# Weights of a two-block transformer kernel laid out unit behind unit in DRAM

## The chip, the core and the metric

The kernel runs on one core of a Trainium2 chip. The metric is the device time of one execution in microseconds (us), from the first to the last instruction.

## What is computed

Two blocks of a transformer run on 256 tokens of width 1024, all in fp32, one behind the other. The first block has two layers: a gated linear attention mixer and a mixture of experts, then a differential attention and a second mixture of experts (4 groups of 4 experts, 512 wide inside). The second block has two layers of feed-forward (2816 wide), a mixer (short convolution, gMLP, sparse attention) and feed-forward again. The parts that matter here are the products with weights:

```python
h = x @ w_in                                   # 1024 x 3088, GLA
for e in range(MOE_EXPERTS):                   # 16 experts, twice
    hdn = silu(t @ w_gate[e]) * (t @ w_up[e])  # 1024 x 512 each
    y = y + combine[:, e:e + 1] * (hdn @ w_down[e])
q1, q2 = split(x @ w_q); kv = x @ w_kv         # 1024 x 1024, 1024 x 2048
swiglu(x, w_gate, w_up, w_down)                # 1024 x 2816, 2816 x 1024, four times
```

Each weight is read from DRAM once. Some 400 MB of weights go through the core in one execution.

## The kernel before

**Units.** All weights are cut into units: up to four rows of k (128 partitions each) by 512 columns, or eight by 256, 1 MB, 2048 fp32 elements for each partition. Some units are smaller: the first product (`q`) has units of two rows of k (512 KB), `kw` has four rows of 280 columns, the low-rank product one unit of 64 KB, the last units of `fdown` two rows. `plan`, `plan_cols`, `plan_split`, `plan_moe` and `plan_ffn` (L308 to L352) make the list `units` with a DRAM view for each unit, and `jobs`, which names the units of each product. L358 to L380 set the order.

**From DRAM to TensorE.** `load_units` (L440) issues one DMA for each unit from the SP queue into one of seven buffers `raw` of 8 KB for each partition. `round_units` (L408, ScalarE, L416) rounds a unit to fp32r into one of four buffers `Whi`. `rest_units` (L420, VectorE, L428; GpSimd L436 for six units) writes the rest `raw - Whi` over `raw` in place and calls it `Wlo`. `use_unit` (L448, TensorE) does three matmuls for each row of k and token tile: high by high (L479), rest by high (L482), high by rest (L487).

**What sets the order.** Every engine runs a program written out by hand. SP waits until unit i-7 is used before it loads unit i; ScalarE waits until unit i has landed and unit i-4 is used. Products on 256 tokens use a unit for two token tiles. The experts of a group work on one tile of 128 gathered tokens, so there a unit is used in half the time. An overflow branch (`over_steps`, L1908) loads the expert weights once more, from GpSimd's queue, if a group has more than 128 tokens.

**In DRAM** the weights lie as the reference has them: row k, then columns. A unit's part for one partition is then four runs of 512 columns (2 KB each), 128 rows of the matrix apart. For the 256-column units of `b_w_q` and `kv_w` it is eight runs of 1 KB, for `kw` four of 1120 bytes. `x_turned` (the tokens, turned and tiled on the host) lies with 4 KB in a row for each partition.

The first product has its own order: SP fetches `x0` (the first half of `x_turned`), the four `q` units, then `x1`, then the rest (L3149 to L3156).

```python
def load_units(sp, a, b):
    for i in range(a, b):
        ap, m, n, _, _ = units[i]
        if i >= NR:
            sp.wait_ge(*on("used", i - NR))
        sp.dma_start(raw[:, i % NR, 0:m * n].rearrange("p (t n) -> p t n", n=n), ap)...
```

Of the kernel before, what the change touches and what calls it, by code (L numbers as in the profile page):

```python
# [18 lines left out]
C_OWN = 1608  # L19
C_SUM = 1616  # L20
C_N = 1640


def constant_table():

    import numpy as np
    t = np.zeros((128, C_N), np.float32)
    i = np.arange(128)
# [104 lines left out]
def build(nc, A, cst_d, out):  # L133
# [14 lines left out]
    def at_(name, shape, dt, off):  # L148
        return nc.alloc_sbuf_tensor_at(name, shape, dt, offset=off)

    def take(nbytes):
        o = base[0]
        base[0] += (nbytes + 31) // 32 * 32
        return o
# [11 lines left out]
    B_o = take(8192)  # L166
    cst_o = take(C_N * 4)

# [11 lines left out]
    gb = at_("gb", [128, 2, 1024], f32, gb_o)  # L180
    cst = at_("cst", [128, C_N], f32, cst_o)

# [90 lines left out]
    where, tenant, held, order, left = {}, {}, set(), list(range(8)), {}  # L273
# [31 lines left out]
    units = []  # L305
    jobs = {}

    def plan(name, view, nk, n, per=None):  # L308

        per = per or max(1, min(nk, 2048 // n))  # L310
        js = []
        k = 0
        while k < nk:
            m = min(per, nk - k)
            js.append(len(units))
            units.append((view[:, k:k + m, :], m, n, k, nk))
            k += m
        jobs[name] = js

    def rows(ap):  # L320
        return ap.rearrange("(t p) n -> p t n", p=128)

    def plan_cols(name, ap, a, b, per=None):
        v = rows(ap)
        plan(name, v[:, :, a:b], v.shape[1], b - a, per)

    def plan_split(name, ap, order=(0, 4)):

        v = rows(ap)
        jobs[name] = [len(units) + i for i in range(4)]  # L330
        for k in order:
            for c in (0, 512):
                units.append((v[:, k:k + 4, c:c + 512], 4, 512, k, 8))

    def plan_moe(l):
        for g in range(4):
            for j in range(4):
                plan_cols(("gate", l, g, j), A["moe_w_gate"][l, 4 * g + j], 0, 512)
                plan_cols(("up", l, g, j), A["moe_w_up"][l, 4 * g + j], 0, 512)
            v = A["moe_w_down"][l, 4 * g:4 * g + 4].rearrange("e (t p) n -> p (e t) n", p=128)  # L340
            for hf in range(2):
                plan(("down", l, g, hf), v[:, :, 512 * hf:512 * hf + 512], 16, 512)

    CH = [(0, 512), (512, 1024), (1024, 1536), (1536, 2048), (2048, 2560), (2560, 2816)]

    def plan_ffn(a, l):
        for c, b in enumerate(CH[:5]):
            plan_cols(("fgate", a, l, c), A[f"{a}_gate_2"][l], *b)
            plan_cols(("fup", a, l, c), A[f"{a}_up_2"][l], *b)
        plan_cols(("fboth", a, l), A[f"{a}_both"][l], 0, 512)  # L350
        for hf in range(2):
            plan_cols(("fdown", a, l, hf), A[f"{a}_down_2"][l], 512 * hf, 512 * hf + 512)  # L352

    GLA_J = [("q", 0, 512), ("lr", 3072, 3088), ("v0", 1024, 1536), ("v1", 1536, 2048), ("k", 512, 1024),
             ("r0", 2048, 2560), ("r1", 2560, 3072)]
    MIX_J = [("kv", 1792, 2304), ("q", 1280, 1792), ("kw", 2304, 2584), ("uv", 768, 1280),
             ("ca", 0, 512), ("cb", 512, 768)]
    for n, a, b in GLA_J:  # L358
        if n == "lr":
            plan(("gla", n), A["low_rank"], 8, 16)  # L360
        else:
            plan_cols(("gla", n), A["a_w_in"][0], a, b, 2 if n == "q" else None)
    plan_split(("gla", "out"), A["a_w_out"][0])
    plan_moe(0)
    for j in range(2):
        c = 256 * j
        plan_cols(("df", 0, j), A["b_w_q"][0], c, c + 256)
        plan_cols(("df", 1, j), A["b_w_q"][0], 512 + c, 768 + c)
        plan_cols(("df", 2, j), A["kv_w"], c, c + 256)
        plan_cols(("df", 3, j), A["kv_w"], 512 + c, 768 + c)  # L370
    for j in range(2):
        plan_cols(("df", "v", j), A["kv_w"], 1024 + 512 * j, 1536 + 512 * j)
    plan_split(("df", "out"), A["b_w_out"][0])
    plan_moe(1)
    for l in range(2):
        plan_ffn("ffn1", l)
        for n, a, b in MIX_J:
            plan_cols(("mx", l, n), A["w_in_2"][l], a, b, 4 if n == "kw" else None)
        plan_split(("mx", l, "out"), A["w_out_2"][l], (4, 0))
        plan_ffn("ffn2", l)  # L380
    NU = len(units)
# [1526 lines left out]
    def over_steps(l):  # L1908

        for g in range(4):  # L1910
            for j in range(4):
                for kind in ("gate", "up"):
                    v = rows(A[f"moe_w_{kind}"][l, 4 * g + j])
                    for k in (0, 4):
                        yield (kind, g, j), v[:, k:k + 4, :], k, 8
            v = A["moe_w_down"][l, 4 * g:4 * g + 4].rearrange("e (t p) n -> p (e t) n", p=128)
            for hf in range(2):
                for k in range(0, 16, 4):
                    yield ("down", g, hf), v[:, k:k + 4, hf * 512:hf * 512 + 512], k, 16

    def over_before(lane, l, v):

# [11 lines left out]
    def overflow_pool(pool, l, place):  # L1934
        P = OVER[l]
        pool.wait_ge(*on("flag", l))
        met = dict(pool.met)
        with pool.taken(flag[0:1, 0:1], f"over{l}_pool", place):
            over_before(pool, l, V_OF[l])
            for i, (name, v, k, nk) in enumerate(over_steps(l)):  # L1940
                if i > 0:
                    pool.wait_ge(*on(P.name, "olo", i - 1))
                pool.dma_start(oraw[:, :].rearrange("p (t n) -> p t n", n=512), v).then_inc(
                    over_landed[l], tick(over_landed[l], P.name, "oraw", i, by=16))
            over_behind(pool, l)
        pool.met = met

    def overflow_act(act, l, place):
        P = OVER[l]
        act.wait_ge(*on("flag", l))  # L1950
        met = dict(act.met)
        with act.taken(flag[0:1, 0:1], f"over{l}_act", place):
            over_before(act, l, V_OF[l])
            for i, (name, v, k, nk) in enumerate(over_steps(l)):
                g = name[1]
                if k == 0 and name == ("gate", g, 0):
                    gather_act(act, P, g, 0)
                    place_turn_act(act, P, g)
                act.wait_ge(*on(P.name, "oraw", i))
                if i > 0:  # L1960
                    act.wait_ge(*on(P.name, "omm", i - 1))
                act.activation(ohi[:, :], oraw[:, :], ACT.Copy).then_inc(P.act, tick(P.act, P.name, "ohi", i))
                if k + 4 == nk and name[0] == "gate":
                    gate_act(act, P, g, name[2], where[(P.name, "out", *name)], (P.name, "out", *name),
                             on(P.name, "omm", i))
                if k + 4 == nk and name[0] == "up":
                    h_turn_act(act, P, g, name[2], ohTh[:, 4 * name[2]:4 * name[2] + 4, :])
                if k + 4 == nk and name[0] == "down":
                    act.wait_ge(*on(P.name, "omm", i))
                    act.wait_ge(*on(P.name, "scat", g - 1, 1, 1) if g else (None, 0))  # L1970
                    act.activation(oY[:, name[2] * 512:name[2] * 512 + 512],
                                   PS[where[(P.name, "out", *name)]][:, :], ACT.Copy).then_inc(
                        P.act, tick(P.act, P.name, "yg", g, name[2]))
                    free(P.act, P.name, "out", *name)
            over_behind(act, l)
        act.met = met
# [1322 lines left out]
```

## Time and profile before

| | |
|---|---|
| median of 3 runs | 1848.53 us (1848.28 to 1849.69) |
| profiled execution, span | 1848.9 us (the profile lists no other time of it) |
| TensorE matmuls (PE) | 1831.4 us busy, 99% |
| weight loads (PEld) | 1524.3 us, 82% |
| VectorE (DVE) | 1301.4 us, 70% |
| ScalarE (ACT) | 1021.1 us, 55% |
| GpSimd (POOL) | 108.5 us, 6% |
| DMA | 426.54 MB, mean 231 GB/s |

A busy TensorE is matmuls in its pipeline; their ends are modelled. "Idle before" in a row names what the engine waited for. A DMA share is the part of a stretch in which packets were under way, as a mean over the core's 16 DMA engines; it can come out a little over 1. The granted clock is the TensorE clock as a share of 2.4 GHz. "To landing" is the time from a DMA's issue to its last byte.

### The profile page before, as it was taken

The numbers are of one execution on the slowest core, as the hardware profiler recorded it, in microseconds if no ns is written. First come the engines' busy times: TensorE is split into PE (matmuls) and PEld (weight loads), VectorE is DVE, ScalarE is ACT, GpSimd is POOL, SyncE is SP. The second block draws the span as 40 slices with busy tenths as digits, with TensorE's granted clock in tenths as the row PEclk, the third lists the DMA queues.
The fourth block names the chain that finished last, engine by engine and source line by source line (L and its number), as shares of the span: only waits on it lengthen the run. The fifth ranks groups of instructions, "written<-read, shape, count | busy, mean of one in ns | idle before, by whom it ended". The sixth has DMA issues, their size and how long they took to land.

```text
span 1848.9 us, 21500 instructions
## 1 busy us (share of the span) xinstructions
PE 1831.4 (99%) x8934; PEld 1524.3 (82%) x8934; DVE 1301.4 (70%) x1335; ACT 1021.1 (55%) x1096; POOL 108.5 (6%) x105
## 2 busy tenths in 40 slices
PE   9999999999999999999999999999999999999998
PEld 7788888888978888887888888888888888888886
DVE  5479999987779999997555667655465546776544
ACT  6548777775757777774443374544254424735432
POOL 1030000000010000000000301100010003020000
PEclk9999999999999999999999999999999999999999
DMA  9548999996447999996555733655565556346551
GB/s 349 171 163 292 355 371 358 355 365 223 137 137 270 356 371 356 358 371 216 184 190 173 231 127 102 227 190 177 171 228 184 180 182 221 114 147 209 190 171 57
DMA packets 216360, 426.54 MB, mean 231 GB/s; under 512 B 7592, under 2 KB 20144, under 8 KB 216256
## 3 DMA queue, kind: packets, MB, share of 16 engines
q1 hardware_dynamic: 210448, 406.93, 63.6%
q0 software_dynamic: 5808, 18.17, 3.1%
q8 instruction: 72, 1.18, 0.3%
q14 instruction: 32, 0.26, 0.0%
HBM read 424.01 MB, written 1.06 MB: 230 GB/s over the span
## 4 chain that ended last, share of the span: by engine, by line
PE 94%; DVE 4%; DMA 1%; ACT 1%; issue 0%; POOL 0%; SPq 0%; ACTq 0%; DVEq 0%
PE ps L487 27%; PE ps L479 26%; PE ps L482 25%; PE ps L609 2%; PE ps L471 2%; PE ps L472 2%; PE ps L2628 1%; DVE Wlo L428 1%; PE ps L1703 1%; PE ps L2529 1%; PE ps L589 1%; PE ps L588 1%; PE ps L587 1%; PE ps L2116 1%; PE ps L2614 1%; DMA raw<-in_kv_w 1%
## 5 line engine op out<-in xcount | busy, mean ns | idle before, releaser
L428 DVE TENSOR_TENSOR Wlo<-raw,Whi 128x2048 fp32r<-128x2048 f32 (+2 forms) x387 | 865.1, 2242 | 400.7 <-ACT Whi L416 400.3
L416 ACT ACTIVATE Whi<-raw 128x2048 fp32r<-128x2048 f32 (+2 forms) x393 | 735.9, 1878 | 470.2 <-PE ps L487 462.3
L487 PE MATMUL ps<-Whi,XTl 128*128 128x512 f32 (+2 forms) x1440 | 536.3, 385 | 0.1
L479 PE MATMUL ps<-Whi,XTh 128*128 128x512 f32 (+2 forms) x1280 | 500.4, 391 | 0.7 <-DVE Wlo L428 0.5
L482 PE MATMUL ps<-Wlo,XTh 128*128 128x512 f32 (+2 forms) x1280 | 494.5, 386 | 0.0
L487 PEld LDWEIGHTS ps<-Whi,XTl 128*128 128x128 f32 x1440 | 269.2, 189 | 53.6 <-DVE XTl L621 0.6
L479 PEld LDWEIGHTS ps<-Whi,XTh 128*128 128x128 f32 x1280 | 241.8, 189 | 49.8 <-issue 3.1
L482 PEld LDWEIGHTS ps<-Wlo,XTh 128*128 128x128 f32 x1280 | 241.9, 189 | 45.9 <-issue 0.2
L479 PE MATMUL ps<-Whi,hTh 128*128 128x512 f32 x352 | 137.6, 391 | 0.0
L487 PE MATMUL ps<-Whi,hTl 128*128 128x512 f32 x352 | 137.1, 389 | 0.0
L482 PE MATMUL ps<-Wlo,hTh 128*128 128x512 f32 x352 | 137.0, 389 | 0.0
L479 PE MATMUL ps<-Whi,mo_hTh 128*128 128x512 f32 x256 | 100.9, 394 | 0.0
L479 PE MATMUL ps<-Whi,XGh 128*128 128x512 f32 x256 | 100.8, 394 | 0.0
L487 PE MATMUL ps<-Whi,XGl 128*128 128x512 f32 x256 | 99.8, 390 | 0.0
L487 PE MATMUL ps<-Whi,mo_hTl 128*128 128x512 f32 x256 | 99.8, 390 | 0.0
L482 PE MATMUL ps<-Wlo,mo_hTh 128*128 128x512 f32 x256 | 99.7, 390 | 0.0
L482 PE MATMUL ps<-Wlo,XGh 128*128 128x512 f32 x256 | 99.7, 389 | 0.0
L487 PEld LDWEIGHTS ps<-Whi,hTl 128*128 128x128 f32 x352 | 66.1, 188 | 13.8
L482 PEld LDWEIGHTS ps<-Wlo,hTh 128*128 128x128 f32 x352 | 66.1, 188 | 13.5
L479 PEld LDWEIGHTS ps<-Whi,hTh 128*128 128x128 f32 x352 | 66.1, 188 | 13.4
L740 POOL TENSOR_TENSOR rs<-rs,cst 128x1 f32<-128x1 f32 x16 | 24.5, 1530 | 891.6 <-DVE rs L713 891.6
L617 ACT ACTIVATE XTh<-ps 128x512 fp32r<-128x512 f32 (+1 forms) x44 | 23.9, 577 | 75.4 <-PE ps L609 75.2
(364 smaller groups left out, 2033.5 us busy)
## 6 DMA issues: line engine op xcount, KB each, us to landing
raw<-in_moe_w_gate SPq DMA_DIRECT2D x64, 1024.0 KB, 5.5
raw<-in_moe_w_up SPq DMA_DIRECT2D x64, 1024.0 KB, 6.0
raw<-in_moe_w_down SPq DMA_DIRECT2D x64, 1024.0 KB, 6.3
raw<-in_ffn_gate SPq DMA_DIRECT2D x40, 1024.0 KB, 5.1
raw<-in_ffn_up SPq DMA_DIRECT2D x40, 1024.0 KB, 5.1
raw<-in_ffn_down SPq DMA_DIRECT2D x40, 1024.0 KB, 5.0
raw<-in_w_in SPq DMA_DIRECT2D x18, 1024.0 KB, 5.4
raw<-in_a_w_in SPq DMA_DIRECT2D x10, 1024.0 KB, 13.9
```

The lines of the kernel that those rows point to most:

```text
L416: act.activation(Whi[:, i % NS, 0:m * n], raw[:, i % NR, 0:m * n], ACT.Copy).then_inc(w_rounded, tick(w_rounded, "rounded", i))
L428: dve.tensor_tensor(Wlo[:, i % NR, 0:m * n], raw[:, i % NR, 0:m * n], h.bitcast(f32), ALU.subtract).then_inc(w_rest, tick(w_rest, "rest", i))
L471: pe.matmul(o, xh(k0 + q, t), h[:, q, :], start=k0 + q == first, stop=False)
L472: pe.matmul(o, xh(k0 + q, t), l[:, q, :], start=False, stop=False)
L479: pe.matmul(o, xh(k, t), h[:, q, :], start=k == first, stop=False)
L482: pe.matmul(o, xh(k, t), l[:, q, :], start=False, stop=False)
L487: x = pe.matmul(o, xl(k, t), h[:, q, :], start=False, stop=k == end)
L587: pe.matmul(o, h[:, q, c], XTh[:, q, :], start=q == 0, stop=False)
L588: pe.matmul(o, h[:, q, c], XTl[:, q, :], start=False, stop=False)
L609: x = pe.transpose(PS[b][:, q * 128:(q + 1) * 128], blk, cst[:, C_ID:C_ID + 128])
L617: act.activation(dst, src, ACT.Copy).then_inc(act_done, tick(act_done, "hi", *name))
L740: pool.tensor_tensor(rs[:, t, 1:2], rs[:, t, 0:1], cst[:, C_ONE + 1:C_ONE + 2], ALU.pow).then_inc(pool_done, tick(pool_done, "root", v, t))
```

## The change

The host lays out each weight unit behind unit, and within a unit partition behind partition, so that one partition's part of a unit is a single run: 8 KB for a 1 MB unit, 4 KB for the `q` units and the last `fdown` units, 4480 bytes for `kw`. `by_units` does this on the host; `unit_of` makes the view of a unit from an offset in the flat array. The units, their order, sizes, buffers and waits are the same. The overflow branch uses the same arrays by the new view. The core of the diff:

```diff
+def by_units(w, a, b, per=None):
+    import numpy as np
+    lead, nk = w.shape[:-2], w.shape[-2] // 128
+    v = w[..., a:b].reshape(*lead, nk, 128, b - a)
+    per = per or unit_rows(nk, b - a)
+    return np.concatenate([np.moveaxis(v[..., k:k + per, :, :], -3, -2).reshape(*lead, -1)
+                           for k in range(0, nk, per)], axis=-1)
...
-    def plan(name, view, nk, n, per=None):
-        per = per or max(1, min(nk, 2048 // n))
+    def plan(name, flat, nk, n, per=None):
+        per = per or unit_rows(nk, n)
...
-            units.append((view[:, k:k + m, :], m, n, k, nk))
+            units.append((unit_of(flat, 128 * k * n, m, n), m, n, k, nk))
...
-    def rows(ap):
-        return ap.rearrange("(t p) n -> p t n", p=128)
+    def unit_of(flat, at, m, n):
+        return flat[at:at + 128 * m * n].rearrange("(p t n) -> p t n", p=128, n=n)
...
-                plan_cols(("gate", l, g, j), A["moe_w_gate"][l, 4 * g + j], 0, 512)
+                plan(("gate", l, g, j), A["moe_w_gate"][l, 4 * g + j], 8, 512)
...
-        plan_cols(("df", 0, j), A["b_w_q"][0], c, c + 256)
+        plan(("df", 0, j), A["b_w_q"][j], 8, 256)
...
-                    for k in (0, 4):
-                        yield (kind, g, j), v[:, k:k + 4, :], k, 8
+                    for k in (0, 4):
+                        yield (kind, g, j), unit_of(v, 65536 * k, 4, 512), k, 8
```

The same is done for `a_w_in`, `a_w_out`, `kv_w`, `b_w_out`, `moe_w_up`, `moe_w_down`, the feed-forward weights, `w_in_2` and `w_out_2`.

## Rows read from the trace of the kernel before

**Rows 1.** The page's head and its busy table (busy us, share, count).
```profile
span 1848.9 us, 21500 instructions
...
PE 1831.4 (99%) x8934; PEld 1524.3 (82%) x8934; DVE 1301.4 (70%) x1335; ACT 1021.1 (55%) x1096; POOL 108.5 (6%) x105
```

**Rows 2.** Windows: length; busy PE, PEld, DVE, ACT, POOL; clock, DMA share, GB/s.
```profile
580.00:840.00 260.00, 260.00 (x1186) 215.35 (x1185) 237.93 (x143) 193.27 (x135) 0.00 (x0) 1.00 1.00 361
860.00:1040.00 180.00, 180.00 (x822) 149.51 (x821) 95.06 (x76) 71.47 (x57) 7.73 (x3) 1.00 0.57 187
```

**Rows 3.** Waits in 580:840, the longest: who, for whom, us, times, longest.
```profile
ACT Whi L416 <- PE ps L487: 45.5, 66, 1.7
```

**Rows 4.** Unit loads (line 445) issued in 580:820, time to landing.
```profile
DMA to landing us min/median/max: 5.1/6.5/7.9
```

**Rows 5.** Waits of ScalarE over the whole span, those for unit loads.
```profile
ACT Whi L416 <- DMA raw<-in_a_w_in: 4.0, 7, 1.5
...
ACT Whi L416 <- DMA raw<-in_b_w_q: 2.8, 2, 1.7
...
ACT Whi L416 <- DMA raw<-in_kv_w: 1.1, 1, 1.1
```

**Rows 6.** Timeline at the start: start us, us, what, idle before and releaser.
```profile
7.79 1.06 ACT L416 ACTIVATE Whi<-raw 128x1024 fp32r<-128x1024 f32 x1 [0.92 <-DMA raw<-in_a_w_in]
...
10.17 0.73 PE L463 MATMUL ps<-Wlo,XTh 128*128 128x512 f32 x2
10.46 1.07 ACT L416 ACTIVATE Whi<-raw 128x1024 fp32r<-128x1024 f32 x1 [0.26 <-DMA raw<-in_a_w_in]
...
11.80 1.15 ACT L634 ACTIVATE XTh<-xs 128x512 fp32r<-128x512 f32 x2 [0.28 <-DMA xs<-in_x_turned]
```

**Rows 7.** DMA issues on the page: count, KB each, median us to landing.
```profile
raw<-in_b_w_q SPq DMA_DIRECT2D x4, 1024.0 KB, 9.8
```

**Rows 8.** Timeline where the expert stages end, first layer, then second.
```profile
417.92 0.39 PE L487 MATMUL ps<-Whi,mo_hTl 128*128 128x512 f32 x1
...
418.50 0.57 ACT L1829 ACTIVATE Ygh<-ps 128x512 fp32r<-128x512 f32 x1
...
840.07 0.39 PE L487 MATMUL ps<-Whi,mo_hTl 128*128 128x512 f32 x1
...
840.49 0.60 ACT L1829 ACTIVATE Ygh<-ps 128x512 fp32r<-128x512 f32 x1 [0.74 <-PE ps L487]
```

**Rows 9.** The mixers of the second block: one window, then matmuls of the timeline.
```profile
1562.00:1574.00 12.00, 12.00 (x73) 11.88 (x72) 4.70 (x5) 6.50 (x13) 0.00 (x0) 0.72 0.26 88
...
1067.50 0.75 PE L2529 MATMUL ps<-mx_kpe,mx_w1v 128*128 128x30 f32 x6
...
1073.71 0.48 PE L479 MATMUL ps<-Whi,XTh 128*128 128x512 f32 x1
...
1563.73 0.75 PE L2529 MATMUL ps<-mx_kpe,mx_w1v 128*128 128x30 f32 x6
...
1573.10 0.48 PE L479 MATMUL ps<-Whi,XTh 128*128 128x512 f32 x1
...
1082.16 0.35 PE L2598 MATMUL ps<-mx_kh,mx_qs 128*128 128x256 f32 x1 [0.52 <-DVE mx_kl L2938]
...
1086.59 0.40 PE L479 MATMUL ps<-Whi,XTh 128*128 128x512 f32 x1
...
1580.81 0.36 PE L2598 MATMUL ps<-mx_kh,mx_qs 128*128 128x256 f32 x1
1583.44 0.39 PE L487 MATMUL ps<-Whi,XTl 128*128 128x512 f32 x1
1583.67 0.39 PE L479 MATMUL ps<-Whi,XTh 128*128 128x512 f32 x1
```

**Rows 10.** DMA packets in 1 to 3.5 us, and the SP queue's on the page.
```profile
DMA packets 157, 0.55 MB, mean 219 GB/s; under 512 B 11, under 2 KB 11, under 8 KB 157
...
q1 hardware_dynamic: 210448, 406.93, 63.6%
```

More of the change, by code:

```diff
@@ L21, with unit_rows @@
 C_N = 1640
+GLA_J = [("q", 0, 512, 2), ("lr", 3072, 3088, None), ("v0", 1024, 1536, None), ("v1", 1536, 2048, None),
+         ("k", 512, 1024, None), ("r0", 2048, 2560, None), ("r1", 2560, 3072, None)]
+MIX_J = [("kv", 1792, 2304, None), ("q", 1280, 1792, None), ("kw", 2304, 2584, 4), ("uv", 768, 1280, None),
+         ("ca", 0, 512, None), ("cb", 512, 768, None)]
+def unit_rows(nk, n):
+    return max(1, min(nk, 2048 // n))
+def by_units(w, a, b, per=None):
[3 more added lines that the diff above has]
+    per = per or unit_rows(nk, b - a)
+    return np.concatenate([np.moveaxis(v[..., k:k + per, :, :], -3, -2).reshape(*lead, -1) for k in range(0, nk, per)],
+                          axis=-1)
 def constant_table():
@@ L315, in plan, with plan_split @@
             js.append(len(units))
-            units.append((view[:, k:k + m, :], m, n, k, nk))
+            units.append((unit_of(flat, 128 * k * n, m, n), m, n, k, nk))
             k += m
         jobs[name] = js
-    def rows(ap):
-        return ap.rearrange("(t p) n -> p t n", p=128)
[L323 to L329, printed above, removed]
+    def unit_of(flat, at, m, n):
+        return flat[at:at + 128 * m * n].rearrange("(p t n) -> p t n", p=128, n=n)
+    def plan_split(name, flat, order=(0, 4)):
         jobs[name] = [len(units) + i for i in range(4)]
         for k in order:
-            for c in (0, 512):
-                units.append((v[:, k:k + 4, c:c + 512], 4, 512, k, 8))
+            for c in range(2):
+                units.append((unit_of(flat, (k // 4 + 2 * c) * 262144, 4, 512), 4, 512, k, 8))
     def plan_moe(l):
@@ L337, in plan_moe @@
             for j in range(4):
-                plan_cols(("gate", l, g, j), A["moe_w_gate"][l, 4 * g + j], 0, 512)
-                plan_cols(("up", l, g, j), A["moe_w_up"][l, 4 * g + j], 0, 512)
-            v = A["moe_w_down"][l, 4 * g:4 * g + 4].rearrange("e (t p) n -> p (e t) n", p=128)
+                plan(("gate", l, g, j), A["moe_w_gate"][l, 4 * g + j], 8, 512)
+                plan(("up", l, g, j), A["moe_w_up"][l, 4 * g + j], 8, 512)
             for hf in range(2):
-                plan(("down", l, g, hf), v[:, :, 512 * hf:512 * hf + 512], 16, 512)
+                plan(("down", l, g, hf), A["moe_w_down"][l, g, hf], 16, 512)
     CH = [(0, 512), (512, 1024), (1024, 1536), (1536, 2048), (2048, 2560), (2560, 2816)]
     def plan_ffn(a, l):
[L347 to L350, printed above, removed]
+        for c in range(5):
+            plan(("fgate", a, l, c), A[f"{a}_gate_2"][l, c], 8, 512)
+            plan(("fup", a, l, c), A[f"{a}_up_2"][l, c], 8, 512)
+        plan(("fboth", a, l), A[f"{a}_both"][l], 8, 512)
         for hf in range(2):
[L352 to L362, printed above, removed]
+            plan(("fdown", a, l, hf), A[f"{a}_down_2"][l, hf], 22, 512)
+    for n, a, b, per in GLA_J:
+        plan(("gla", n), A[f"a_w_in_{n}"], 8, b - a, per)
     plan_split(("gla", "out"), A["a_w_out"][0])
@@ L365, in build @@
     for j in range(2):
-        c = 256 * j
-        plan_cols(("df", 0, j), A["b_w_q"][0], c, c + 256)
-        plan_cols(("df", 1, j), A["b_w_q"][0], 512 + c, 768 + c)
-        plan_cols(("df", 2, j), A["kv_w"], c, c + 256)
-        plan_cols(("df", 3, j), A["kv_w"], 512 + c, 768 + c)
+        plan(("df", 0, j), A["b_w_q"][j], 8, 256)
+        plan(("df", 1, j), A["b_w_q"][2 + j], 8, 256)
+        plan(("df", 2, j), A["kv_k"][j], 8, 256)
+        plan(("df", 3, j), A["kv_k"][2 + j], 8, 256)
     for j in range(2):
-        plan_cols(("df", "v", j), A["kv_w"], 1024 + 512 * j, 1536 + 512 * j)
+        plan(("df", "v", j), A["kv_v"][j], 8, 512)
     plan_split(("df", "out"), A["b_w_out"][0])
@@ L376, in build @@
         plan_ffn("ffn1", l)
-        for n, a, b in MIX_J:
-            plan_cols(("mx", l, n), A["w_in_2"][l], a, b, 4 if n == "kw" else None)
+        for n, a, b, per in MIX_J:
+            plan(("mx", l, n), A[f"w_in_2_{n}"][l], 8, b - a, per)
         plan_split(("mx", l, "out"), A["w_out_2"][l], (4, 0))
@@ L1912, in over_steps @@
                 for kind in ("gate", "up"):
-                    v = rows(A[f"moe_w_{kind}"][l, 4 * g + j])
+                    v = A[f"moe_w_{kind}"][l, 4 * g + j]
                     for k in (0, 4):
-                        yield (kind, g, j), v[:, k:k + 4, :], k, 8
-            v = A["moe_w_down"][l, 4 * g:4 * g + 4].rearrange("e (t p) n -> p (e t) n", p=128)
+                        yield (kind, g, j), unit_of(v, 65536 * k, 4, 512), k, 8
             for hf in range(2):
+                v = A["moe_w_down"][l, g, hf]
                 for k in range(0, 16, 4):
-                    yield ("down", g, hf), v[:, k:k + 4, hf * 512:hf * 512 + 512], k, 16
+                    yield ("down", g, hf), unit_of(v, 65536 * k, 4, 512), k, 16
     def over_before(lane, l, v):
@@ L3264 @@
     inputs["x_turned"] = x[0].reshape(2, 128, 8, 128).transpose(0, 3, 2, 1)
-    inputs["low_rank"] = inputs["a_w_in"][0][:, 3072:].reshape(8, 128, 16).transpose(1, 0, 2)
+    for n, a, b, per in GLA_J:
+        inputs[f"a_w_in_{n}"] = by_units(inputs["a_w_in"][0], a, b, per)
+    for n, a, b, per in MIX_J:
+        inputs[f"w_in_2_{n}"] = by_units(inputs["w_in_2"], a, b, per)
+    kv_w, b_w_q = inputs.pop("kv_w"), inputs.pop("b_w_q")[0]
+    del inputs["a_w_in"], inputs["w_in_2"]
+    inputs["b_w_q"] = np.stack([by_units(b_w_q, c, c + 256) for c in range(0, 1024, 256)])
+    inputs["kv_k"] = np.stack([by_units(kv_w, c, c + 256) for c in range(0, 1024, 256)])
+    inputs["kv_v"] = np.stack([by_units(kv_w, c, c + 512) for c in (1024, 1536)])
+    for k in ("gate", "up"):
+        inputs[f"moe_w_{k}"] = by_units(inputs[f"moe_w_{k}"], 0, 512)
+    down = inputs["moe_w_down"].reshape(2, 4, 2048, 1024)
+    inputs["moe_w_down"] = np.stack([by_units(down, c, c + 512) for c in (0, 512)], axis=2)
     w = np.concatenate([inputs.pop("moe_w_group"), inputs.pop("moe_w_router")], axis=2)
@@ L3269 @@
     for f in ("ffn1", "ffn2"):
-        inputs[f"{f}_both"] = np.concatenate([inputs[f"{f}_{k}_2"][:, :, 2560:] for k in ("gate", "up")], axis=2)
+        both = np.concatenate([inputs[f"{f}_{k}_2"][:, :, 2560:] for k in ("gate", "up")], axis=2)
+        inputs[f"{f}_both"] = by_units(both, 0, 512)
+        for k in ("gate", "up"):
+            w = inputs[f"{f}_{k}_2"]
+            inputs[f"{f}_{k}_2"] = np.stack([by_units(w, c, c + 512) for c in range(0, 2560, 512)], axis=1)
+        w = inputs[f"{f}_down_2"]
+        inputs[f"{f}_down_2"] = np.stack([by_units(w, c, c + 512) for c in (0, 512)], axis=1)
     for name in inputs:
@@ L3288 @@
             a = np.concatenate([a[:, :512], c], axis=1)
+        if name in ("a_w_out", "b_w_out", "w_out_2"):
+            a = np.concatenate([by_units(a, c, c + 512) for c in (0, 512)], axis=-1)
         a = np.ascontiguousarray(a)
```

## The prediction, made before the changed kernel was run

> **What bounds the kernel now.** I read the page's busy table first: TensorE is busy 1831.4 of 1848.9 us [rows 1], so 17.5 us is all the time in which it does nothing, from any cause. The chain of waits gives PE 94% and DMA 1% of the span. The transfers look just as full in one place: in the expert stages (150 to 400 and 580 to 840 us) the DMA share is 1.00 at 361 GB/s, beside a TensorE that is busy for 260.00 of 260 us [rows 2]. Two full resources can't both be the limit, and three readings say which is. First, who waits: in 580:840 ScalarE's rounding of a unit (L416, the first reader of `raw`) waits 45.5 us, 66 times, for matmuls to give a buffer back, and never for a DMA [rows 3]. Second, the pace: 1186 matmuls in 260 us are 219 ns each, and in the feed-forward stage, where the DMAs carry only 187 GB/s at share 0.57, 822 in 180 us are 219 ns each as well [rows 2]. Doubling the traffic doesn't slow TensorE, and halving it doesn't speed it up. Third, what the same 16 engines do when asked for more: at the start three transfers of 512 KB end within 4.01 us, from 7.79 to 11.80 [rows 6], 524,288 bytes / 1.337 us = 392 GB/s. So the expert stages take 361 GB/s because TensorE frees no more buffers, at 92% of what the queue has shown. They are bound by TensorE.
>
> **The change, part by part.** It removes and adds no instruction on any engine, no wait and no byte. `load_units` issues the same units in the same order behind the same `used` waits; only the DRAM side of each view becomes one run. Matmuls, L416, L428 and L436 read the same SBUF bytes. So every term is the landing of some unit where something waits for it, and the wait table of ScalarE names all such places: 4.0 us behind `in_a_w_in`, 2.8 behind `in_b_w_q`, 1.1 behind `in_kv_w` [rows 5]. That is 7.9 us of ScalarE, not of TensorE.
>
> *Expert stages, 2 x some 265 us.* ScalarE takes unit i when unit i-4 is used, SP issues it when unit i-7 is used: a lead of 3 units. A unit of one token tile is 4 x 3 matmuls of 0.227 us (the rows at full clock in [rows 9] step by that), 2.72 us, so the lead is 8.2 us, and landings take 5.1 / 6.5 / 7.9 us (least, median, most) [rows 4]. All of them are in time now. Landing earlier gains 0; landing later costs nothing up to 0.3 us for the worst and 1.7 us for the median.
>
> *Start.* The `q` units of two k-rows land 1.33 us apart: ScalarE starts on the second at 7.79 and on the fourth at 10.46, both straight out of a wait for the DMA [rows 6]. TensorE's part of such a unit is 2 x 3 matmuls, 1.36 us, so DMA and TensorE keep step here, and TensorE first runs without a gap from 10.17 us, when VectorE's rest of the second unit is there [rows 6]. What moves that point is the landing of the second unit. Ahead of it lie `x_turned[0]` (not changed) and two units of 512 KB, 2 x 1.33 = 2.66 us of transfer that become runs of 4 KB instead of 2 KB. What does that save? The next transfer in the same queue, `x_turned[1]`, is 512 KB in runs of 4 KB already, and ScalarE gets it at 11.80, 1.34 us after the last `q` unit [rows 6]. Twice the run, the same time: 0, or 0.02 lost if the 0.01 is real for both units. The other end is all of ScalarE's wait for the second unit, 0.92 us [rows 6]: with that gone ScalarE itself would be late next. The row of `x_turned[1]` is the same kind of transfer in the same queue, so I stay near its end and take 0.1 gained.
> The Trainium skill (DMA: Bandwidth & Descriptors, Why small descriptors are slow) has a fixed cost of about 3 beats of 32 bytes per packet. An estimate from that page: 67 beats for 2 KB against 131 for 4 KB, 2% of 2.66 us, 0.06 us. Rows 6 show none of it, and the sum is the same with either.
> The later `a_w_in` waits (the remaining ScalarE waits of at most 1.5 us each [rows 5]) fall in 20 to 43 us, where TensorE has no gap over what the 10.17 start set; they cost nothing now and return nothing.
>
> *End of the first expert stage.* Here the units of `b_w_q` and `kv_w` have runs of 1 KB and take 9.8 us to land (median of the four `in_b_w_q`) [rows 7], over the lead of 8.2. ScalarE waits, its roundings slip, and the copy of the last expert product (L1829) stands behind one: it starts 0.58 us after the last matmul's start (417.92 to 418.50). At the end of the second expert stage, where the next units are `ffn1` with 2 KB runs and no DMA wait is seen, the same copy starts 0.42 us after it (840.07 to 840.49) [rows 8]. With 8 KB runs these units should land like the others, and the first case becomes the second: 0.16 us gained, at most 0.3 if the norm behind it also tightens, at least 0. I take 0.15. What is late next is the matmul itself.
>
> *Everything else* (first mixer, attention, feed-forward, both later mixers, the tail): no wait for `raw` stands in the table, the lead is longer (two token tiles per unit), gain 0. The overflow branch reads by the new view too, but isn't taken (no instruction of it is in the trace), 0. POOL's small loads share the 16 engines; they may wait behind longer packets, but `gb` and the router weights are asked for a stage ahead, 0.
>
> **Sum:** 1848.9 - 0.1 - 0.15 = 1848.65 us of span. No time of the profiled execution itself is listed beside its span; the median of the three runs is 1848.53, 0.37 below the span, so I go by the same distance: 1848.3 us.
>
> **The rivals.**
> *A, the clock falls move.* TensorE's granted clock is 1.00 nearly everywhere, but in 1562:1574 its mean is 0.72 [rows 9]: the engine, which had just run many short matmuls of 30 columns, goes on at 1.2 GHz for a while. The same code in layer 0 stays at 2.4 GHz. From the L2529 group to the next 512-column L479 is 6.21 us in layer 0 (1067.50 to 1073.71) and 9.37 in layer 1 (1563.73 to 1573.10): the fall costs 3.16 us. A second fall is in layer 0, after short matmuls and a gap of 0.52 us: L2598 to the seventh L479/L482/L487 behind it is 4.43 us (1082.16 to 1086.59) against 2.86 in layer 1 (1580.81 to 1583.67): 1.57 us. Each site falls in one layer and not in the other, so they are near a border and a shift of a few tenths of a us may tip them. Without both: 1848.3 - 4.7 = 1843.6. With each in both layers: 1848.3 + 4.7 = 1853.0. One site alone moves 1.6 or 3.2 and stays inside what counts as no change. Against: the three runs lie within 1.4 us.
> *B, the expert stages are DMA-bound after all.* Then 550 us at 361 GB/s would go at 392 or better: 550 x (1 - 361/392) = 43 us less, about 1805. For it: share 1.00 [rows 2], and that busy time of matmuls is modelled. Against: [rows 3], and equal pace with half the traffic.
> The Trainium skill (Perfetto Trace Analysis, DMA Optimizations) says that going from 2 KB to 4 or 8 KB can dramatically improve throughput and calls it the primary step when bandwidth use is high and the kernel DMA-bound. The first half of the condition holds here, the second doesn't; this rival is that rule.
> *C, slower: long runs land later in the expert stages.* The runs of neighbouring partitions now start 8 KB apart in DRAM in place of 2 or 4 KB, and each is four times as long. If the sustained rate falls under the 361 GB/s that TensorE asks for, the landings pass 8.2 us and each unit waits. It decides at 361 GB/s; per 1% below, 550 us grow by 5.5. At 355 GB/s (1.7% short): + 9, about 1857. For it: the worst landing is only 0.3 us inside the lead [rows 4], and no raw load with runs of 8 KB is in the trace. Against: the step from 1 KB to 2 KB runs helped (9.8 to 6.5 us [rows 4, 7]), the one from 2 to 4 KB changed nothing [rows 6].
> *D, the descriptors don't get longer.* A view with three dimensions could still be cut at 512 elements. Then nothing changes: 1848.5. Against: in 1 to 3.5 us, when mainly `x_turned[0]` is moved, which is 8 x 128 elements in a row, 157 packets carry 0.55 MB, 3.5 KB each [rows 10], so contiguous dimensions are joined.
>
> **Chances.** Forecast 0.84 (single clock sites within it); A 0.06, half each way; B 0.03; C 0.05; D 0.02. A measurement of this kernel can tell 0.2%, 3.7 us, from no change. Faster by more: A's half and B, 0.06; slower by more: A's half and C, 0.08; same: 0.86. The range takes in one clock site each way: 1848.3 - 3.2 = 1845.1 and 1848.3 + 3.2 = 1851.5; I keep 1845.0 to 1851.3.
>
> **What would show it.** The SP queue's 210448 packets for 406.93 MB [rows 10] become some 50,000 of 8 KB plus several thousand small ones; unchanged packets would be D. In 580:840 TensorE busy for all of it and ScalarE's waits on matmuls still about 45 us: right. ScalarE waits for `raw` transfers there, or landings over 8.2 us: C. GB/s in that stretch above 361 with fewer us per expert: B. The `in_b_w_q` and `in_kv_w` waits gone and L1829 0.42 us behind its matmul: the second term. The gapless start at about 10.1 instead of 10.17 us: the first. A different clock row in the mixers: A. I am wrong if the time moves by over 3.7 us without such a clock row.

## The result: 25 us slower, nearly all of it in two places where no weight was late

The changed kernel takes 1873.61 us (median of 4 runs, 1871.75 to 1875.49) against 1848.40 (4 runs, 1846.08 to 1849.69): ratio 1.0139, 95% interval 1.0126 to 1.0151. I had forecast 1848.3 and a range that ends at 1851.3.

From the page of the changed kernel: head, busy table, DMA packets, and the SP queue's own line:

```profile
span 1873.7 us, 21500 instructions
...
PE 1850.8 (99%) x8934; PEld 1543.0 (82%) x8934; DVE 1301.4 (69%) x1335; ACT 1021.8 (55%) x1096; POOL 108.7 (6%) x105
...
DMA packets 63784, 426.54 MB, mean 228 GB/s; under 512 B 7592, under 2 KB 7856, under 8 KB 15552
...
q1 hardware_dynamic: 57872, 406.93, 59.8%
```

The same bytes go in 57872 packets of the SP queue instead of 210448 [rows 10], so the runs did get longer. VectorE and ScalarE are busy as long as before; TensorE is "busy" 19.4 us longer with the same 8934 matmuls [rows 1]. More busy time for the same work is the first hint at its clock.

The expert stages did not change. Here are the window, ScalarE's wait for buffers and the landings of the unit loads in the changed kernel (its line numbers are 8 higher: L445 is L453):

```profile
580.00:840.00 260.00, 260.00 (x1185) 215.30 (x1184) 238.57 (x143) 193.00 (x135) 0.00 (x0) 1.00 0.96 361
...
ACT Whi L424 <- PE ps L495: 45.5, 66, 1.7
...
DMA to landing us min/median/max: 4.7/4.9/6.2
```

The landings are 1.6 us shorter at the median [rows 4] and nobody gains from it: still 260.00 busy, 361 GB/s, 45.5 us, 66 times [rows 2, 3].

Since both kernels issue the same matmuls in the same order, their starts can be compared one by one. In the first mixer of the second block, up to the first matmul of L2529 (L2537 now), the changed kernel is only 0.6 us late: the matmul in front of it starts at 1059.72, and in the old kernel at 1059.08. The timeline of the changed kernel from there on:

```profile
1059.72 0.29 PE L487 MATMUL ps<-Whi,XTh 128*128 128x280 f32 x1
1063.69 0.60 PE L2537 MATMUL ps<-mx_kpe,mx_w1k 128*128 128x30 f32 x2 [3.69 <-DMA mx_glg<-in_gmlp_ln_b]
...
1079.35 1.32 PE L2537 MATMUL ps<-mx_kpe,mx_w1v 128*128 128x30 f32 x6
...
1089.30 0.48 PE L487 MATMUL ps<-Whi,XTh 128*128 128x512 f32 x1
...
1099.90 0.39 PE L487 MATMUL ps<-Whi,XTh 128*128 128x512 f32 x1
...
1572.17 0.61 PE L2537 MATMUL ps<-mx_kpe,mx_w1k 128*128 128x30 f32 x2 [3.26 <-DMA mx_glg<-in_gmlp_ln_b]
...
1597.83 0.49 PE L487 MATMUL ps<-Whi,XTh 128*128 128x512 f32 x1
```

TensorE waits 3.69 us for `mx_glg`, the last load of a group on **GpSimd's** queue. It waits for something that it does not read. Its matmul reads `mx_w1k`, which was asked for at 1042.6 us and took 7.1 us to land; `mx_glg` is first read by VectorE, at 1126 us. But all loads of the group share one semaphore (the counter that a reader waits on), so the first reader waits for the last load.

Six short matmuls then take 1.32 us; in [rows 9] six of them (1067.50) took 0.75. Against [rows 9] the lateness is 11.85 us at 1079.35 and 15.59 at 1089.30. At 1099.90 it is 13.31, since the short fall of the clock that the old kernel had in between, and the gap of 0.52 us before it, are gone. The second mixer goes the same way: 3.26 us of wait, and 24.73 late at 1597.83 (1573.10 in [rows 9]). From there to the last matmul (1865.89 against 1841.13) it stays 24.8. So 12.7 us are lost in the first mixer, 11.4 in the second, 0.6 elsewhere. The two waits are 7.0 us of this; the windows of the two stretches say what the other 17 are (the last three columns are granted clock, DMA share and GB/s):

```profile
1063.00:1088.00 25.00, 24.31 (x112) 24.34 (x113) 5.65 (x6) 6.13 (x9) 0.00 (x0) 0.52 0.22 79
1571.00:1596.00 25.00, 23.83 (x108) 23.86 (x109) 5.65 (x6) 5.93 (x10) 0.00 (x0) 0.52 0.22 81
```

A mean of 0.52 over 25 us is 24 us at 1.2 GHz. The DMA share of 0.22 says that the transfers are mostly idle meanwhile.

The group lands late because its loads take longer. Time from issue to landing of the two `mx_glg` loads in both mixers, the old kernel first, the changed one second:

```profile
DMA to landing us min/median/max: 8.1/8.5/9.0
```

```profile
DMA to landing us min/median/max: 13.0/13.2/13.8
```

In the old kernel the last one, issued at 1049.11, is there at 1058.1; the first matmul that needs the group starts at 1059.20. The margin was 1.1 us, and no table of waits shows it, as no one waits. In the changed kernel the same load takes 13.8 us in place of 9.0, 4.8 more.

Theory T, formed from this: the 16 DMA engines take packets of the two queues in turn, so four times longer packets on the SP queue make GpSimd's group land later; the wait lets the clock fall, and through the short matmuls behind it the clock stays down. It has two rivals. By P the stretches at 1.2 GHz come from the long packets and not from the wait. By L it is the place in DRAM that makes the group late and not the length of a run.

### The profile page after: what moved, and what is told of

It is laid out like the page before. It is cut to its first block, busy times and chain, and to the rows that moved or that the text cites. A ratio compares the mean times of both kernels' runs of the same rounds, so it can differ in the third digit from the quotient of the medians.

```text
span 1873.7 us, 21500 instructions
## 1 busy us (share of the span) xinstructions
PE 1850.8 (99%) x8934; PEld 1543.0 (82%) x8934; DVE 1301.4 (69%) x1335; ACT 1021.8 (55%) x1096; POOL 108.7 (6%) x105
## 3 DMA queue, kind: packets, MB, share of 16 engines
q1 hardware_dynamic: 57872, 406.93, 59.8%
## 4 chain that ended last, share of the span: by engine, by line
PE 92%; DVE 4%; DMA 2%; POOL 2%; ACT 0%; issue 0%; SPq 0%; DVEq 0%; POOLq 0%; ACTq 0%
PE ps L495 26%; PE ps L487 25%; PE ps L490 25%; PE ps L617 2%; DMA mx_glg<-in_gmlp_ln_b 1%; PE ps L2537 1%; PE ps L479 1%; PE ps L480 1%; PE ps L2636 1%; DVE Wlo L436 1%; PE ps L1711 1%; PE ps L597 1%; PE ps L596 1%; PE ps L595 1%; PE ps L2124 1%; PE ps L2622 1%
```

## The experiments

In every comparison "before" is the old kernel, run on the same chip in the same rounds.

**1. Only the wait, no packet changed.** The old layout; before it issues the group's loads GpSimd does three `pow` instructions whose result nobody uses, as a delay:

```diff
         point[("pein", l)] = point[("landed", "pein")]
+        for _ in range(3):
+            pool.tensor_tensor(dly[:, 0:1], cst[:, C_ONE:C_ONE + 1], half(1), ALU.pow)...
         fetch(pool, "mx", M.w1[0][:, :, :], ...)
```

> The old layout everywhere. In front of the mixer's group of loads on GpSimd's queue (mx_w1k to mx_glg) stand three small GpSimd powers, 1.53 us each by the rows of L740, so the group is issued and lands 4.6 us later with no packet of any DMA changed. Theory T (the changed kernel is slower because this group lands 4.6 us late: TensorE waits at the first L2529 matmul, and the clock falls after the wait and stays down through the short matmuls behind it): a wait of about 3.6 us in front of L2529 in both mixers, two stretches of some 24 us at 1.2 GHz, 1872 us. Rival P (only the wait comes from the late landing, the long stretches at 1.2 GHz come from the long packets themselves): the same wait, 2 x 3.6 us, clock as before, about 1856 us. If neither holds: 1848.

Measured: 1873.85 us against 1846.83, ratio 1.0144 (1.0127 to 1.0161). Waits in front of L2534 (the same matmul) in the two mixers, and the windows behind them:

```profile
PE ps L2534 <- DMA mx_glg<-in_gmlp_ln_b: 4.1, 1, 4.1
...
PE ps L2534 <- DMA mx_glg<-in_gmlp_ln_b: 3.8, 1, 3.8
...
1063.00:1088.00 25.00, 25.00 (x124) 24.95 (x125) 5.87 (x7) 7.20 (x14) 0.00 (x0) 0.56 0.26 85
1571.00:1596.00 25.00, 25.00 (x124) 25.00 (x124) 5.87 (x7) 6.92 (x12) 0.00 (x0) 0.55 0.26 92
```

The old layout with a late group is as slow as the changed kernel, and has the same two stretches at 1.2 GHz. Long packets are not needed for them. P falls.

**2. Only the mixers' weights.** The old layout with `w_in_2` alone, the first weights of the two mixers, unit behind unit. These are 22 unit loads:

```diff
-            plan_cols(("mx", l, n), A["w_in_2"][l], a, b, 4 if n == "kw" else None)
+            per, flat, js = per or unit_rows(8, b - a), A[f"w_in_2_{n}"][l], []
...
+                units.append((flat[at:at + 128 * m * (b - a)].rearrange("(p t n) -> p t n", p=128, n=b - a), ...
```

> The old layout with only w_in_2, the first weights of the two mixers, unit behind unit (22 of the 383 or so unit loads, those that are in flight while GpSimd's group lands). T: the whole loss comes back from these few loads: GpSimd's group 13 us to landing for its last load, wait 3.5 us, about 1872 us. Rival P, or any loss that is spread over all loads: near 1850 us. The start is that of the old layout, so 0.3 us less than the changed kernel there.

Measured: 1871.91 us against 1846.83, ratio 1.0129 (1.0112 to 1.0146); `mx_glg` 13.0 to 14.0 us to landing, waits of 3.9 and 3.4 us. The intervals of this ratio and of the changed kernel's overlap: these 22 loads alone bring the loss.

**3. All but these.** The changed kernel with `w_in_2` in the old layout.

```diff
-            plan(("mx", l, n), A[f"w_in_2_{n}"][l], 8, b - a, per)
+            plan_view(("mx", l, n), A["w_in_2"][l].rearrange("(t p) n -> p t n", p=128), a, b, per)
```

> The changed kernel with only w_in_2 back in the old layout, all other loads in runs of 8 KB. T: the last load of GpSimd's group lands in about 8.5 to 9 us again, no wait at L2537, no long stretch at 1.2 GHz, 1848 to 1849 us. Rival P: with 8 KB packets everywhere else the clock or the experts still lose, 1855 us or more.

Measured: 1847.15 us against 1846.83, ratio 0.9998 (0.9989 to 1.0008). One landing of `mx_glg` took 10.3 us and TensorE waited 0.2 us, with no fall behind it: the clock is 1.00 up to 1083 us, where the short fall of the old kernel stands.

**4. Late loads that no one waits for.** The changed kernel; the three large loads, which are issued first and read first, get a semaphore of their own. TensorE waits on that one, and so does VectorE before it reads `mx_gw` (the same edit there is left out below):

```diff
-        fetch(pool, "mx", M.gwT[:, :, :], A["gmlp_w_2"][l])
...
+        fetch(pool, "mxw", M.gwT[:, :, :], A["gmlp_w_2"][l])
+        point[("mxw", l)] = point[("landed", "mxw")]
...
-                    pe.wait_ge(*on("mx", l))
+                    pe.wait_ge(*on("mxw", l))
```

> The changed kernel, all runs of 8 KB. The three large loads of GpSimd's group (mx_w1k, mx_w1v, mx_gw) get a semaphore of their own; TensorE (L2534) and VectorE (L2927) wait on that one, the other readers on the whole group as before. T: the loads still land late (mx_glg about 13 us), but mx_gw lands at some 1057.7 us and TensorE comes at 1060, so no wait, no long stretch at 1.2 GHz, 1847 to 1850 us. Rival P: the wait of 3.7 us goes and the long stretches at 1.2 GHz stay, about 1866 us.

Measured: 1848.01 us against 1846.83, ratio 1.0005 (0.9995 to 1.0014). `mx_glg` still takes 12.9 to 13.1 us; `mx_gw`, issued at 1044.4, lands 13.3 us later at 1057.7, and nothing waits. The windows of the same stretches:

```profile
1059.00:1083.00 24.00, 23.48 (x175) 22.20 (x174) 14.17 (x15) 16.73 (x26) 0.00 (x0) 1.00 0.55 185
1555.00:1579.00 24.00, 23.48 (x172) 22.05 (x172) 14.31 (x16) 15.94 (x25) 0.00 (x0) 1.00 0.53 186
```

The clock is 1.00 with every run at 8 KB, and the 25 us are back, by an edit to the waits alone. Together with the first experiment this settles P from both sides: the wait without long packets costs the 25 us, long packets without the wait cost nothing that can be told from noise.

**5. Unit behind unit, but runs of 2 KB.** Each unit is one piece of 1 MB in DRAM; inside it k comes before the partition. `r` is how many rows of k one partition has in one run; here it is 1 for 512 columns. The host lays the arrays out to match (left out):

```diff
-        return flat[at:at + 128 * m * n].rearrange("(p t n) -> p t n", p=128, n=n)
+        r = pieces(0, m, n)[0][1]
+        v = flat[at:at + 128 * m * n]
+        if r == 1:
+            return v.rearrange("(t p n) -> p t n", p=128, n=n)
+        return v.rearrange("(u p r n) -> p u r n", p=128, r=r, n=n)
```

> Unit lies behind unit as in the change, each 1 MB unit in one piece of DRAM, but inside a unit the order is row of k, then partition: every run is 2 KB again. T in its full form (an engine takes packets of the two queues in turn, so the length of the SP queue's packets decides how fast GpSimd's group gets through): the last load of the group lands in 8.5 to 9 us as in the old layout, no wait at L2537, 1847 us. Rival L (where the weights lie in DRAM makes the group late, not how long the runs are): group late by 4 us or more, 1872 us.

Measured: 1847.56 us against 1847.91, ratio 1.0007 (0.9993 to 1.0021); `mx_glg` 8.2 to 10.1 us, within what it took in the third experiment (7.9 to 10.3), and no wait. The place alone does nothing. L falls.

**6. Runs of 4 KB.** The same with two rows of k together: the last line of the edit above, with r = 2 for 512 columns.

> As the kernel before this one with two rows of k for each partition together: runs of 4 KB. T: the lateness of GpSimd's group grows with the packets. 2 KB gave 9.0 us for mx_glg in the first mixer, 8 KB 13.8; on a line over the packet length 4 KB gives about 10.6. TensorE comes 10.3 us after the issue (1059.4 against 1049.1), so the wait is some 0.3 us in place of 3.7, and there is no long stretch at 1.2 GHz: 1847 to 1850 us. If the lateness saturates at 4 KB: 1870.

Measured: 1868.20 us against 1847.91, ratio 1.0100 (1.0081 to 1.0118). Landings 10.3 to 12.4 us, waits of 1.3 and 2.3 us. The direction is T's, but I had expected 1847 to 1850 us and missed twice. The last load came 1 to 2 us later than a line over the packet length gives, and a wait of 1.3 us was already followed by a long stretch at 1.2 GHz (window of the first mixer):

```profile
1061.00:1083.00 22.00, 22.00 (x108) 22.00 (x108) 5.27 (x6) 6.21 (x10) 0.00 (x0) 0.53 0.29 103
```

The three packet lengths also show the turns. First the packets of both queues from 1044 us to the group's landing (q1 is the SP queue, q0 GpSimd's; packets, MB, share), at 2 KB (1044 to 1058), 4 KB (to 1061) and 8 KB (to 1063):

```profile
q0 software_dynamic: 942, 2.72, 66.0%
q1 hardware_dynamic: 833, 1.67, 35.6%
```

```profile
q0 software_dynamic: 939, 2.71, 52.9%
q1 hardware_dynamic: 767, 2.99, 46.9%
```

```profile
q1 hardware_dynamic: 449, 3.29, 51.0%
q0 software_dynamic: 942, 2.72, 46.9%
```

GpSimd's 940 packets go through in all three. The SP queue's are 833, 767 and 449 in number, but 1.67, 2.99 and 3.29 MB. These windows also hold time in which only one of the queues has work: up to 1049 us GpSimd's is nearly alone in all three. The turns are seen where both have work, at 2 KB in 1051 to 1056 us, at 4 KB in 1051 to 1057, at 8 KB in 1051 to 1060:

```profile
q1 hardware_dynamic: 448, 0.91, 55.2%
q0 software_dynamic: 441, 0.81, 50.6%
```

```profile
q1 hardware_dynamic: 387, 1.52, 67.8%
q0 software_dynamic: 377, 0.68, 35.0%
```

```profile
q1 hardware_dynamic: 359, 2.68, 77.5%
q0 software_dynamic: 354, 0.83, 24.7%
```

One packet of one queue passes for one of the other at every length, whatever they carry: 1.02, 1.03 and 1.01 to one. The smaller total of 449 at 8 KB comes from the times outside: from 1060 to 1063 us the SP queue moves 66 packets and GpSimd's 175. The Trainium skill (DMA: Bandwidth & Descriptors, Queues, rings and completion order) says that each DMA engine goes round between its queues at packet granularity; by these counts the trace agrees. What the profile counts as a packet is one run here; whether the page's packet is the same thing no run shows.

How much this delays the group is an estimate: at 8 KB the extra 1.62 MB of the SP queue at the old kernel's 314 GB/s are 5.2 us, against 4.8 measured. At 4 KB the same sum gives 4.2 us, against 2.5 measured (11.5 us for the last load in this mixer), so the estimate is rough.

**7. The separate semaphore in the old layout.** The edit of the fourth experiment.

> The old layout with the separate semaphore for the three large loads. No reader waits for the group in the old layout, so T and P both expect no change: 1846 to 1849 us. It tells whether the separate semaphore brings anything by itself that would hide a remaining cost of the changed layout in e4_ownsem.

Measured: 1848.08 us against 1847.91, ratio 1.0005 (0.9995 to 1.0014). The separate semaphore brings nothing by itself, so it hid no remaining cost in the fourth experiment.

**8. The wait filled with work.** The changed kernel; in both mixers 17 matmuls on constants stand in front of the wait:

```diff
                     pe.wait_ge(*on("kpe", l))
+                    for _ in range(17 if i == 0 else 0):
+                        pe.matmul(PS[where["hg", l, i]][:, :], idr[:, :], bc(mkr[:, 0:1], (0, 4), (1, 128)), ...)
                     pe.wait_ge(*on("mx", l))
```

> The changed kernel; in front of the wait for GpSimd's group TensorE does 17 matmuls of 512 columns on constants, 17 x 0.227 = 3.9 us, as much as it waits there. The group is as late as in the changed kernel, but TensorE is busy meanwhile. T, with the clock as an effect of the idle time: no long stretch at 1.2 GHz, and only the 3.9 us themselves are lost in each mixer, 1847 + 7.8 = 1855 us. If the late group or the mixture of packets brings the clock down by itself: 1872 us.

Measured: 1858.11 us against 1847.91, ratio 1.0050 (1.0033 to 1.0067). The timeline of the first mixer, and a window of each:

```profile
1059.41 4.06 PE L2535 MATMUL ps<-mkr,idr 128*128 128x512 f32 x17
1063.51 0.41 PE L2540 MATMUL ps<-mx_kpe,mx_w1k 128*128 128x30 f32 x2
...
1063.96 0.75 PE L2540 MATMUL ps<-mx_kpe,mx_w1k 128*128 128x30 f32 x6
```

```profile
1059.00:1083.00 24.00, 23.96 (x151) 22.53 (x151) 8.57 (x8) 11.27 (x17) 0.00 (x0) 0.86 0.40 125
...
1555.00:1580.00 25.00, 25.00 (x172) 23.18 (x170) 11.50 (x19) 11.17 (x16) 0.00 (x0) 1.00 0.57 205
```

TensorE comes to the short matmuls as late as in the changed kernel (1063.51 against 1063.69), but busy, and six of them take 0.75 us again. In the second mixer the clock does not fall at all in this stretch. In the first it falls for a short time from about 1072 us on (mean clock 0.86 in the window), which I had not expected and which stays unexplained. The changed kernel's 25 us become 10: 2 x 3.9 us of filler, and some 2 us for that fall. The 15 us between the two kernels are, roughly, what the lower clock behind an idle wait costs; the timeline of the changed kernel gave 17.

**9 and 10. How long a wait it takes.** The first experiment with one (9) and with two (10) of the delaying instructions.

> The old layout with one GpSimd power (1.53 us) in front of the mixer's group of loads. Three of them moved the landing from 1058.1 to about 1062.4 us, so one should move it by 1.4 us to about 1059.5, against TensorE's arrival at 1059.2: a wait of 0 to 0.5 us. T, clock as an effect of the length of the wait: too short for a stretch at 1.2 GHz (0.2 us in e3_mixold gave none), 1847 to 1850 us. If any wait there is enough: 1867.

> The same with two powers: landing 2.9 us later, about 1061.0 us, a wait of some 1.8 us in each mixer. With runs of 4 KB waits of 1.3 and 2.3 us were followed by 20.5 us at 1.2 GHz each and cost 20 us. T: the same here with every weight in runs of 2 KB, about 1868 us. If long packets are needed for the stretch at 1.2 GHz after a short wait: 1847 + 3.6 = 1851 us.

Measured: with two (10), 1870.44 us against 1847.84, ratio 1.0107 (1.0071 to 1.0143), waits of 2.1 us each. With one (9), 1854.49 us, ratio 1.0030 (1.0004 to 1.0056), with single runs from 1848.11 to 1864.52; neither my 1850 nor 1867. In its profile the waits were 0.9 and 1.1 us, longer than the 0 to 0.5 I had worked out, and the two mixers answered differently:

```profile
PE ps L2534 <- DMA mx_glg<-in_gmlp_ln_b: 0.9, 1, 0.9
...
PE ps L2534 <- DMA mx_glg<-in_gmlp_ln_b: 1.1, 1, 1.1
```

```profile
1059.00:1083.00 24.00, 23.08 (x126) 22.84 (x125) 6.53 (x8) 9.40 (x15) 0.00 (x0) 0.64 0.41 145
...
1560.00:1584.00 24.00, 22.93 (x163) 21.16 (x161) 13.03 (x11) 14.35 (x24) 0.00 (x0) 1.00 0.66 218
```

After the wait of 0.9 us the clock was low for most of the stretch, after that of 1.1 us not at all. A wait of about 1 us at this place can go either way, one of 2 us or more was followed by the fall each time (eight of eight: the changed kernel, experiments 1, 2 and 10), and so were those of 1.3 and 2.3 us at 4 KB.

The fall need not come at once. Behind five of these eight waits TensorE's next matmuls are slow from the first, behind the other three they slow down within 1.5 us. Behind the wait of 0.9 us, which ended at 1060.17, six of them still take 0.75 us, and those of 1063.89 take 1.32:

```profile
1060.60 0.75 PE L2534 MATMUL ps<-mx_kpe,mx_w1k 128*128 128x30 f32 x6
...
1063.89 1.32 PE L2534 MATMUL ps<-mx_kpe,mx_w1k 128*128 128x30 f32 x6
```

Since the old kernel also has falls in these stretches with no such wait [rows 9], the single fall of experiment 9 is not shown to come from its wait. For the waits of 2 us and more, eight of eight leave little doubt.

## Why the prediction was wrong

**The step that failed** is the term "Everything else", which I put at 0: "POOL's small loads share the 16 engines; they may wait behind longer packets, but `gb` and the router weights are asked for a stage ahead, 0." That term measured 24.1 us. I named the right cause, priced it by two loads with long leads, and never asked for the third group of the same queue. The mixer's group is asked for at 1042 to 1050 us, while SP fills its buffers with the mixer's weights, and wanted at 1059.20: 10.1 us behind the last issue, of which the landing took 9.0. My test for a place at risk was ScalarE's wait table: "the wait table of ScalarE names all such places". It names where something is late already. Of the things that are not late it says nothing, and it was read for `raw` alone, though the change touches every packet that shares an engine with `raw`. So it was not the size of a term that was off: no term of the sum let a late load of another queue delay TensorE, and none had the lower clock behind such a wait, which is 17 of the 24.1 us.

**The expert stages.** Right: bound by TensorE, 260.00 of 260 us, landings well inside the lead. Rival C (long runs land later) is refuted, they land sooner (6.5 to 4.9 us). Rival B (DMA-bound) too: the DMA share fell to 0.96 and the pace stayed. Rival D (the descriptors don't get longer) is refuted by the 57872 packets. B and C were priced with 550 us of expert stages, where the text has 2 x 265; that changes neither.

**The start.** I took 0.1 us of gain from the spacing of `x_turned[1]`. ScalarE's starts on the `q` units are now 8.09, 9.36 and 10.62:

```profile
8.09 1.06 ACT L424 ACTIVATE Whi<-raw 128x1024 fp32r<-128x1024 f32 x1 [1.36 <-DMA raw<-in_a_w_in_q]
9.36 1.06 ACT L424 ACTIVATE Whi<-raw 128x1024 fp32r<-128x1024 f32 x1 [0.21 <-DMA raw<-in_a_w_in_q]
10.62 1.06 ACT L424 ACTIVATE Whi<-raw 128x1024 fp32r<-128x1024 f32 x1 [0.20 <-DMA raw<-in_a_w_in_q]
```

The spacing did shrink, 1.26 us against 1.33 [rows 6], but the second unit came 0.3 later, and TensorE first runs without a gap from 10.46 instead of 10.17. Among the runs of the old layout that point moves as much (9.56 in experiment 7), so neither sign is shown.

**The end of the first expert stage.** The copy L1829 (L1837) now starts 0.42 us after its matmul, as forecast [rows 8]:

```profile
418.30 0.39 PE L495 MATMUL ps<-Whi,mo_hTl 128*128 128x512 f32 x1
...
418.72 0.60 ACT L1837 ACTIVATE Ygh<-ps 128x512 fp32r<-128x512 f32 x1 [0.74 <-PE ps L495]
```

TensorE got the 0.16 us and lost them again. Its lateness is 0.38 us at the matmul in front (418.30 against 417.92) and 0.24 at the matmul that reads the copy (419.46 against 419.22). Right behind it six matmuls of L2086 take 4.54 us where the old kernel's took 2.84, in a short stretch at 1.2 GHz (mean clock 0.91 in 412 to 424 us, 1.00 in the old kernel), and at 427 us the lateness is 0.6. What set off this fall no run tests.

**Rival A** had half of the mechanism. I took the clock falls for a lottery of a few us and priced them at 4.7 at most, from the falls that the old trace happens to have. The first site of [rows 9] lies in the same run of short matmuls, and with a fall at its beginning it costs not 3 us but 11. I had the row that says so (30-column matmuls follow a low clock) and did not ask what a real wait in front of them would do. The lottery itself is also larger than I took it for: single runs of the old kernel beside the later experiments took up to 1856.85 us at a mean clock of 0.993, against a median of 1847.84 and clocks of mostly 0.998. My last sign of being wrong was a change by over 3.7 us without a different clock row in the mixers. The change came with such rows, so that sign would not have caught it.

**The level.** I put the time 0.37 us below the span. The profiled execution of the changed kernel took 1875.49 us with a span of 1873.7, so the time is about 1.8 us above the span. By that distance the profiled execution of the old kernel took about 1850.7 us, some 2 us more than the median of its kernel. Beside the 25 us this is small.

No version ran faster than the old kernel: experiments 3, 4, 5 and 7 all tie with it.

## What to carry to other kernels

Before changing the size or order of transfers on one queue, list the loads of every other queue that are in flight beside them, and for each the time between its landing and the first wait for it. Here a margin of 1.1 us was used up, and no wait table had shown it. Let loads that are read first have a semaphore apart from those that are read later, so that the first reader does not wait for the last load. Price a new wait of TensorE by what runs behind it: in front of many short matmuls a wait of 3.7 us cost 12.7 us, and 15.0 without the short fall that went away.

## What the runs showed of the hardware

- While two queues both have work, their packets pass one for one and not byte for byte: 448 beside 441 with runs of 2 KB on the SP queue, 387 beside 377 with 4 KB, 359 beside 354 with 8 KB. So the queue with the longer packets takes the bandwidth, 2.68 MB beside 0.83 in the last case. GpSimd's load of 1 MB (`mx_w1v`) went from 10.3 to 12.6 us to landing, while the SP queue's units landed sooner.
- 8 KB runs land a 1 MB unit in 4.9 us where 2 KB runs took 6.5, both at 361 GB/s of demand.
- TensorE's clock fell to 1.2 GHz behind every idle wait of 2 us and more in front of the short matmuls: eight of eight, five of them with the first matmul already slow and three within 1.5 us, and the wait of 2.3 us at 4 KB too. In the profile of experiment 9 it was down from 1063 us on, 2.8 us after the end of a wait of 0.9 us, and it stayed at 2.4 GHz behind one of 1.1 us. With constant matmuls in place of the wait of 3.7 us the short matmuls behind them ran at 2.4 GHz.
- Once down it stayed down for 24 us with TensorE busy 24.31 of 25 us, in matmuls of which 64 of 112 had 30 columns, and it was back at 2.4 GHz within the run of 280-column matmuls behind them. The same code entered without the wait ran through at 2.4 GHz in experiment 4.
